# A float32 transformer block on one core: who makes the weight sums of the seven-product pairs, and when

## The reference

```python
hf = rms_norm(x, g_ffn)
x = x + (silu(hf @ w_gate) * (hf @ w_up)) @ w_down
```

## Time and profile before

| | us |
|---|---|
| median of 3 runs | 2406.77 (2404.95 to 2407.11) |
| profiled execution | 2403.7 |
| its span | 2401.9 |
| TensorE busy | 2371.4 |
| VectorE busy | 1888.3 |
| ScalarE busy | 1189.5 |
| GpSimd busy | 29.7 |

### The profile page before, as it was taken

How to read it: one execution, slowest core, us unless ns; L and a number is a source line. 1 busy time by engine, 2 the same in 40 slices (tenths; PEclk the granted TensorE clock), 3 DMA queues, 4 the chain that set the end, 5 groups by cost and what they waited for, 6 DMA issues and landing times.

```text
span 2401.9 us, 30801 instructions
## 1 busy us (share of the span) xinstructions
PE 2371.4 (99%) x10764; PEld 1970.5 (82%) x10764; DVE 1888.3 (79%) x2614; ACT 1189.5 (50%) x1615; POOL 29.7 (1%) x50
## 2 busy tenths in 40 slices
PE   9999999999999999999999999999999999999999
PEld 8988888888788888788888888888878888878887
DVE  7788887888578866778897977978857886677885
ACT  6554555544444544545554445554444454454553
POOL 1000000000000000000000000000000000000000
PEclk9999999999999999999999999999999999999999
DMA  8655455655555555555555564665555655555655
GB/s 307 234 168 190 160 178 184 201 188 194 182 188 193 193 184 202 184 176 201 184 193 193 188 211 159 198 219 186 193 184 184 201 188 190 193 188 181 202 190 169
DMA packets 126495, 462.24 MB, mean 192 GB/s; under 512 B 13712, under 2 KB 14352, under 8 KB 125728
## 3 DMA queue, kind: packets, MB, share of 16 engines
q1 hardware_dynamic: 116736, 421.32, 52.9%
q0 software_dynamic: 9344, 38.85, 4.7%
q10 hardware_dynamic: 288, 0.33, 0.0%
HBM read 458.35 MB, written 2.10 MB: 192 GB/s over the span
## 4 chain that ended last, share of the span: by engine, by line
PE 98%; issue 1%; DVE 0%; ACT 0%; DMA 0%; SPq 0%; ACTq 0%; DVEq 0%
PE acc L586 67%; PE pt L586 11%; PE po L586 10%; PE acc L734 2%; PE pt L734 2%; PE po L734 1%; PE acc L935 1%; PE acc L591 1%; PE po L918 1%; PE acc L849 1%; PE po L910 1%; PE pt L889 0%; PE acc L864 0%; PE acc L623 0%; PE pt L675 0%
## 5 line engine op out<-in xcount | busy, mean ns | idle before, releaser
L1598 DVE TENSOR_TENSOR w_lo<-raw,w_hi 128x1024 fp32r<-128x1024 f32 x796 | 965.7, 1223 | 441.8 <-ACT w_hi L1090 435.3
L1090 ACT ACTIVATE w_hi<-raw 128x1024 fp32r<-128x1024 f32 x795 | 833.4, 1058 | 893.0 <-PE acc L586 573.2
L586 PE MATMUL acc<-w_hi,norm_hi 128*128 128x512 f32 (+1 forms) x1524 | 593.4, 390 | 0.1
L586 PE MATMUL acc<-w_hi,norm_lo 128*128 128x512 f32 (+1 forms) x1524 | 590.2, 388 | 0.0
L586 PE MATMUL acc<-w_lo,norm_hi 128*128 128x512 f32 (+1 forms) x1524 | 404.5, 387 | 0.0
L586 PEld LDWEIGHTS acc<-w_hi,norm_hi 128*128 128x128 f32 x1524 | 286.1, 188 | 58.3 <-issue 0.8
L586 PEld LDWEIGHTS acc<-w_hi,norm_lo 128*128 128x128 f32 x1524 | 286.2, 188 | 57.6
L586 PEld LDWEIGHTS acc<-w_lo,norm_hi 128*128 128x128 f32 x1524 | 285.0, 188 | 58.3
L586 PE MATMUL acc<-w_hi,mix_hi 128*128 128x512 f32 x848 | 331.1, 390 | 0.5 <-ACT w_hi L1396 0.4
L586 PE MATMUL acc<-w_hi,mix_lo 128*128 128x512 f32 x848 | 330.0, 389 | 0.0
L586 PE MATMUL acc<-w_lo,mix_hi 128*128 128x512 f32 x848 | 226.8, 389 | 0.0
(11 more groups left out here) (312 smaller groups left out, 2361.5 us busy)
## 6 DMA issues: line engine op xcount, KB each, us to landing
raw<-stream SPq DMA_DIRECT2D x795, 512.0 KB, 3.4
heads<-seven_in POOLq DMA_DIRECT2D x24, 1024.0 KB, 6.7
heads<-x_in POOLq DMA_DIRECT2D x4, 512.0 KB, 6.7
x<-x_tok POOLq DMA_DIRECT2D x4, 512.0 KB, 7.3
x<-mem_tok POOLq DMA_DIRECT2D x2, 1024.0 KB, 6.9
x<-x_tok POOLq DMA_DIRECT2D x1, 2048.0 KB, 9.1
heads<-rows_in POOLq DMA_DIRECT2D x2, 1024.0 KB, 8.6
heads<-decay_in POOLq DMA_DIRECT2D x4, 512.0 KB, 5.2
```

The source lines that it names most:

```text
L586: last = pe.matmul(out_[:, c * NB:c * NB + width], a[:, k * T + c * P:k * T + (c + 1) * P], w[:, s, kk * width:(kk + 1) * width], start=cl ...
L1090: act.activation(w_hi[:, (units.fixed - 1) % RING, :], src, ACT.Copy).then_inc(w_hi_ready, 1)
L1598: dve.tensor_tensor(w_lo[:, s, :], src, w_hi[:, s, :].bitcast(F32), ALU.subtract)\
```

## The change

GpSimd makes the four sums, straight behind the DMA of the tiles, with a semaphore and a wait of its own between them. They leave VectorE's list. VectorE's low halves move forward by one split (by two in the short down pair); the preparation's offset to the sums stays as an argument, `behind`. ScalarE's high halves and copies move forward only in the short down pair, by one split. VectorE's combination moves forward by one split in most pairs. TensorE opens a pair behind the fourth unit of the running up pair's second block, where it was the third, if the running pair is itself one with seven products; openings in down pairs stay.

```diff
+        pool_done = sem("pool_done")
...
+            def after_own(ins, n):
+
+                ins.then_inc(pool_done, 1)
+                pool.wait_ge(pool_done, n)
+
+            def seven_sums(j):
+
+                pool.wait_ge(seven_landed, 16 * (j + 1))
+                after_own(pool.tensor_tensor(raw7(T3), raw7(W22), raw7(T1), ALU.subtract), 3 * j + 1)
+                after_own(pool.tensor_tensor(raw7(T1), raw7(T1), raw7(W11), ALU.subtract), 3 * j + 2)
+                after_own(pool.tensor_tensor(raw7(T2), raw7(W22), raw7(T1), ALU.subtract), 3 * j + 3)
+                pool.tensor_tensor(raw7(T4), raw7(W21), raw7(T2), ALU.subtract).then_inc(seven_summed, 1)
...
                 load_seven(j)
+                seven_sums(j)
...
                             one_block(NU - 1, norm, k0=UK, token_major=True, opened=True,
-                                      mid=opening(pair, 2))
+                                      mid=opening(pair, 3))
...
# ScalarE, down pairs
-                            steps(2 * nd - 2, both(turned_, preparing(after, 6 if p == 0 else 5),
-                                                   joining(after, 2 * nd - 5 if nd > 6 else 9)))
+                            steps(2 * nd - 2, both(turned_, preparing(after, 6 - p if nd > 6 else 4),
+                                                   joining(after, 2 * nd - 5 if nd > 6 else 8)))
...
# VectorE
-            def seven_sums(j):
-
-                dve.wait_ge(seven_landed, 16 * (j + 1))
-                dve.tensor_tensor(raw7(T3), raw7(W22), raw7(T1), ALU.subtract)
-                link(dve.tensor_tensor(raw7(T1), raw7(T1), raw7(W11), ALU.subtract))
-                link(dve.tensor_tensor(raw7(T2), raw7(W22), raw7(T1), ALU.subtract))
-                dve.tensor_tensor(raw7(T4), raw7(W21), raw7(T2), ALU.subtract).then_inc(seven_summed, 1)
...
-                def preparing(j, at):
+                def preparing(j, at, behind=3):
...
-                    return {at: [lambda: seven_sums(j)], at + 3: [lambda: seven_lo(j, 0)],
-                            at + 4: [lambda: seven_lo(j, 1)]}
+                    return {at + behind: [lambda: seven_lo(j, 0)],
+                            at + behind + 1: [lambda: seven_lo(j, 1)]}
...
-                            ready_ = joining(after, 12)
+                            ready_ = joining(after, 11)
...
-                            steps(2 * NU - 2, both(early, preparing(after, 4), sums, ready_, ends_))
+                            steps(2 * NU - 2, both(early, preparing(after, 3), sums, ready_, ends_))
...
-                            ready_ = both(preparing(after, 5), joining(after, 2 * k - 2))
+                            ready_ = both(preparing(after, 4), joining(after, 2 * k - 3))
...
-                            ready_ = both(preparing(after, 4), joining(after, 2 * k - 2 if k > 5 else 9))
+                            ready_ = both(preparing(after, 3, 3 if k > 5 else 2), joining(after, 2 * k - 3 if k > 5 else 8))
```

## The result

| | before | changed |
|---|---|---|
| median | 2405.86 us (2404.64 to 2407.11, 4 runs) | 2374.44 us (2372.77 to 2376.75, 4 runs) |
| ratio | | 0.987, interval 0.9853 to 0.9887 |
| profiled execution, span | 2403.7, 2401.9 | 2376.75, 2375.0 |

The medians differ by 31.4 us, the spans of the two profiled executions by 26.9: the profiled execution of before (2403.7) was 2 us under its median, that of the changed kernel 2 us above.

The account below looks back on a forecast made before the run. TensorE was taken as the bound, busy 2371.4 of 2401.9 us. Removing 31.5 us of its stalls gave a 2370.4 span, 2372.2 with 1.8 around it; from the median 2375.3, said as 2375, range 2371 to 2386.

Parts of the forecast that it names:

- What TensorE waits for: Before the seven-product matmuls (line 734), 23.8 of TensorE's 30.5 us idle; the openings wait for VectorE's low halves.
- the 1.27 stalls: Five TensorE waits of 1.27 us per MLP before a pair's first products, each costing 1.55 us by DMA spacing.
- What the stalls cost in full: Per MLP 5 x 1.55 + 0.57 + 7.44 = 15.76 us, both 31.5, read from the spacing of GpSimd's seven-tile DMAs.
- The GpSimd chain: Four sums on GpSimd behind the tiles' landing: 1.16 us each plus semaphores and port waits, 6.5 us.
- VectorE's waits for GpSimd "at nothing": VectorE splits delayed 1.2 to 1.5 us, at most four times a pair, costed at nothing; failure would show at line 586.
- The first pair's sums run while VectorE is far from them: At the first pair, GpSimd's sums were to meet no VectorE work, so nothing is delayed.
- Short pair: Ten-unit pair, 39.39 us to become 31.95; no stall if the sums end by 614.1, a chain of 8.3 us.
- Rival A: GpSimd chain of 8.3 to 14.7 us: short pairs' openings stall again; 2379.3 at 10 us, 2390 at the end; chance 0.17.
- Rival B: Chain from 14.7 us: ScalarE's weight split late, TensorE stalls at line 586 one for one; 2492 at 20 us; chance 0.07.
- the first cause of the late low halves: VectorE reaches the four sums only at 741.23, ending 743.97; ScalarE sits 3.04 us for them and hands over late.
- the low halves' queueing: On VectorE, low halves stand behind the eleventh unit's split, for which VectorE waits 2.24 us on ScalarE.
- this alone already removes the 1.27 stall: Regular pair: low halves one split earlier, sums' time gone, run 745.2 to 747.5; TensorE could open at 752.6.

Follow-up runs that it names:

- the long chain: Changed kernel in which GpSimd runs the first sum nine times instead of once, a chain of 12 sums; 2587.09 us (one run).
- with fills: Kernel before, with four GpSimd fills of a 128x512 tile added per pair, VectorE's sums waiting for them; 2403.34 us, ratio 0.9994.
- the extra subtractions: Kernel before, with four GpSimd subtractions of the sums' shape added per pair, VectorE's sums waiting for them; 2436.95 us, ratio 1.0136.

## Why the prediction was right, point by point

- **What TensorE waits for**: right. Two separate edits, each of which lets the low halves end before the opening, took the 1.27 stalls away.
- **What the stalls cost in full** (31.5 us, by the spacing of the DMAs instead of by the idle time): right. The kernels without any of them stand 31.1 to 34.5 us under before; the idle sum of 23.8 would have been too little. By the spacing of the DMAs each MLP was to give 15.76; it gave 14.7 and 15.0 and kept 0.95 and 0.62 in its short pair. What a lower clock costs behind a stall is seen in the long chain.
- **The GpSimd chain**, 6.5 us: measured 6.3 in the median, 6.2 to 8.1. A part was off: 1.29 us a sum rather than 1.16.
- **VectorE's waits for GpSimd "at nothing"**: TensorE lost nothing by them in 23 pairs; in the first pair the step "The first pair's sums run while VectorE is far from them" failed. VectorE is beside them, working on the normalised input, and TensorE lost 2.4 us (1.5 in the other profiled execution). It showed as the prediction had said a failure would, as waits of TensorE at the unit line, now 602. Three short operations each lost 1.03 us and a split 0.89, where I had thought of splits only. The kernels with the sums put later or away, and with fills, show it. The Trainium skill's "SBUF — State Buffer", section "Who interferes with whom", states the exclusion, for reads and not for GpSimd's writes; the traces agree: 4.79 against 1.67 us beside sums, 1.67 beside fills.
- **Short pair**: the limit was right, the landing wasn't. I took 6.7 us from issue to landing; it was 8.5 there (602.06 to 610.56), inside the 5.7 to 10.1 of the earlier trace rows, and with a chain of 7.1 the sums ended 15.9 us into the pair, for a limit of 15.3. The stall is 0.69. In the second MLP the excess and the stall were both 0.3. Rival A (0.17) had such a stall, but from a chain over 8.3; here the landing made it.
- **Rival B**: right in place and in its one for one, as the long chain showed, and in its threshold as far as a line carried back from longer chains can show it. Its price, 117 us lost at a chain of 20, was too small against the 213 of the long chain (20.6): the stalls were longer than 5.3 us, the short pairs' openings stalled for 10, and the lower clock behind each stall was left out.
- **What each part brings**: the prediction let the sums' place on VectorE stand as the first cause of the late low halves. It is a cause in the old order (2386.71 against 2403.48 with the sums moved alone), but with both jobs one split earlier it need not leave VectorE (2371.95 and 2372.09). The prediction named the low halves' queueing as the second reason, and said of their new place that "this alone already removes the 1.27 stall", but it worked that out with the sums already on GpSimd. The kernel with the order alone was not among its cases. The hit (2375 for 2374.44) is in part luck: 2405.86 less 31.5, plus the 2 to 4 us lost beside GpSimd and in the short pairs, is 2376 to 2378; the scatter of the medians covers the rest.

Why the changed kernel's first profiled execution is 2 us above its other runs can be read from its second one, whose span is 2.3 us shorter (2372.7). The first MLP's start accounts for 0.9 (88.92 and 88.03), each short pair for 0.6 (32.90 and 32.57 against 32.30 and 31.96), the rest of the span for 0.2. In the short pairs the tiles landed 8.5 and 8.1 us behind their issue in the first execution, 7.7 and 6.7 in the second. In the first MLP they landed earlier in the first execution (8.3 against 9.9), so the sums caught the weight split as well. What stays open is why the landings vary.

## What to carry to other kernels

Before work is moved to another engine, ask whether its place in the order is what is late. Here a few jobs moved by one or two places among the weight splits gave all of it; the engine change gave nothing more and cost 2 us. A stall of the bound engine is priced by the spacing of something periodic behind it, not by the idle time shown; and where GpSimd reads SBUF, put it beside VectorE's transposes or idle time, not beside two-input operations that are late.

## What the runs showed of the hardware that was not expected

- Two-input operations of VectorE and GpSimd's sums take turns: operations of 0.48 us became 1.51 us each beside sums that followed one another, a split of 1.23 up to 2.35, a sum of 1.29 up to 2.28. A GpSimd fill of the same tile (0.53 us) disturbed nothing, and VectorE's transposes beside the extra subtractions kept their 0.43 to 0.44 us (450.45 to 452.24).
- Behind the 2.97 stall of the kernel before, matmuls came at 0.43 us instead of 0.23 for some 3.5 us, behind the 6.5 us stalls of the long chain for some 4. It is not certain behind each: with the later opening alone, the short pair of the first MLP took 39.40 us and the second 37.79, with the same two stalls of 2.97 and 2.32 in both; the granted clock was 0.91 around the first and 1.00 around the second.
